# Two transposes of the identity in place of four at each settling place of a two-block transformer kernel

## The chip, the cores and the metric

The kernel runs on one core of one Trainium2 chip. The metric is the device time of one execution in microseconds, the median of the runs. All data are 32-bit floats; the large products are made with TensorE's fp32r type from operands that are split into a high and a low part.

## The reference, cut to what matters

One sequence of 256 tokens with 2048 channels passes two blocks. The first has a gated linear attention, a dilated window attention and a product-key expert layer; the second has a pooling layer and a linear recurrence, each with gates and an output projection.

```python
xn = rms_norm(x, norm1_g)
h = xn @ w_in                                  # then attention parts of h
x = x + mixed @ w_out
...
u = expert_down[ib]                            # first block: all 16384 experts, with gates
act = gelu(einsum('tkd,td->tk', u, xb))
x = x + einsum('tk,tkd->td', gb * act, expert_up[ib])
...
for i in range(2):                             # second block: pooling, then recurrence
    uz = rmsnorm(x, g_pre[i]) @ w_in[i]
    y = pool_mixer(u) or rglru(conv(u))
    o = (y * silu(z)) @ w_out[i]
    x = x + rmsnorm(o, g_post[i])
    gate = sigmoid(rmsnorm(x, g_ple_in[i]) @ w_ple_gate[i])
    x = x + rmsnorm((p[i] @ w_ple[i]) * gate, g_ple_out[i])
```

The kernel computes the expert layer densely: every expert's activation for every token, times a gate that is zero for the experts that a token didn't choose.

## The kernel before, in words

All weights come as 589 chunks of 128 x 2048 numbers (1 MB), in one written-out order. SyncE issues the load of each chunk into one of three raw buffers (RAW). ScalarE rounds a chunk to its high part (WH, L1050), VectorE subtracts to get the low part (WL, L1555). Both parts have three slots; a few chunks have extra ones (WX). The activations stand transposed and split in the same way, k-tile by k-tile, high part and low part, in A, M, CO, DD, P or Y.

TensorE works through the chunks in order. A chunk is 16 blocks of 128 x 128 weights. For each block the function `block` issues three matmuls of 256 columns, each with its own weight load: high weights times high activations (L558), high weights times low activations (L559), low weights times high activations (L560). The prediction calls these three a triple, and the 16 triples (48 matmuls) of a chunk a tile. A tile's 16 blocks are added in one half of a PSUM bank. The weight load of the next matmul runs while the current one streams.

The chunk numbers of the stages: 0 to 12 gated linear attention, 13 to 48 dilated attention, 49 to 64 output projection, 65 to 80 queries, 81 to 152 and 225 to 280 the first ("down") products of the experts, 153 to 224 and 281 to 336 the second ("up") products, 337 to 416 the pooling layer's inputs, 417 to 448 its output projection, 449 to 450 and 451 to 466 its gate, 467 to 538 the recurrence's inputs, 539 to 570 its output projection, 571 to 588 the last gate.

Other work for TensorE is put between triples by hand: transposes and products of the attention heads (among them L718 and L719, two 512-column products with ones; L726, two transposes; L742, four transposes), the score products and the index transposes of the top-k stage (L839, L847), the gate products (L857), and the sums over channels by a product with ones (`summed`, L599, L601, L604).

At 24 places TensorE also makes transposes of the identity matrix, L573, by the function `settle`. Their output goes to the upper half of the bank whose lower half the next tile will fill; nobody reads it. The set SETTLE names 22 of them by chunk: 53, 68, 84, 105, 119, 129, 138, 147, 150, 227, 229, 344, 346, 361, 381, 401, 458, 474, 486, 504, 522 and 580. There the transposes stand ahead of the tile's first triple, behind the waits for the bank and for the chunk's low part. The other two are in the output projections, ahead of the second tile of each (chunks 418 and 540).

Of the kernel before, what the change touches and what calls it, by code (L numbers as in the profile page):

```python
# [12 lines left out]
T = 256  # L13
# [70 lines left out]
def build(nc, d, out):  # L84
# [483 lines left out]

    def settle(e, b):

        for i in range(4):
            at = T + i % 2 * 128
            e.transpose(BANK[b][:, at:at + 128], IDENT[:, :], IDENT[:, :])  # L573

    def tile(e, c, x):

        wait_bank(e, c)
        e.wait_ge(s_lo, c + 1)
        if c in SETTLE:
            settle(e, bank[c])  # L580
        for b in range(16):
            ins = block(e, psum(c), c, b, x, b, b == 0, b == 15)
            if b == 15:
                ins.then_inc(s_used, 1)
            yield b
# [336 lines left out]
    def pe_oproj(e, l):  # L922

        c0, n = C_O[l], LEAD[l]
        for hf in range(2):
            for i in range(n):
                c = c0 + n * hf + i
                if hf == 0:
                    wait_bank(e, ("o", l, i))
                    if l and i == 4:  # L930
                        e.wait_ge(RA.sem, RA.at(("ig", 7)))
                e.wait_ge(s_lo, c + 1)
                if hf == 0 and i == 1:
                    settle(e, bank["o", l, i])
                for b in range(16):
                    if i == 0:
                        wait_y(e, l, 16 * hf + b)
                    ins = block(e, psum(("o", l, i)), c, b, Y, 16 * hf + b, hf == b == 0, hf == 1 and b == 15)
                ins.then_inc(s_used, 1)
        for i in range(n, 16):  # L940
            wait_bank(e, ("o", l, i))
            for hf in range(2):
                c = c0 + 2 * i + hf
                e.wait_ge(s_lo, c + 1)
                for b in range(16):
                    ins = block(e, psum(("o", l, i)), c, b, Y, 16 * hf + b, hf == b == 0, hf == 1 and b == 15)
                ins.then_inc(s_used, 1)
# [1454 lines left out]
```

## Time and profile before

| | before |
|---|---|
| time, median of 3 runs | 3403.35 us |
| lowest and highest run | 3401.82 and 3406.58 us |
| the profiled execution's span | 3399.5 us |
| median less span | 3.85 us |
| PE (matmuls) busy | 3377.7 us |
| DVE busy | 2285.7 us |
| ACT busy | 1663.9 us |
| L573, the transposes of the identity | 96 instructions |

The span is measured from the first to the last instruction of one profiled execution, the run's time is that of whole executions; a single time of the profiled execution beside its span was not recorded, so the median stands beside it. PE's busy time counts matmuls that overlap, so a share near 100% says that a matmul was always under way, not how many there were. How many triples begin in a stretch of time is to be read from the start times and the counts.

### The profile page before, as it was taken

To read this page: it belongs to the slowest core of one execution; us is meant where nothing else is said; L and a number is where in the kernel's file an instruction comes from. 1 tells how busy PE (TensorE), PEld (TensorE's weight loads), DVE (VectorE), ACT (ScalarE), POOL (GpSimd) and SP (SyncE) were. 2 spreads that over 40 slices of the span, in tenths; PEclk is the share of its full clock that TensorE was granted. 3 is DMA by queue.
4 is the path that set the end of the run, shared out by engine and by line. 5 is a ranking of instruction groups with operands and counts; after the bars stand their busy time and mean duration, and the time that the engine had idled before them with its cause. 6 is when DMAs were issued, how large, how long until landed. Compare 5 with 4: busy or idle time off the path is not lost.

```text
span 3399.5 us, 66556 instructions
## 1 busy us (share of the span) xinstructions
PE 3377.7 (99%) x29384; PEld 3355.2 (99%) x29384; DVE 2285.7 (67%) x3023; ACT 1663.9 (49%) x1789; POOL 134.9 (4%) x132
## 2 busy tenths in 40 slices
PE   9999999999999999999999999999999999999999
PEld 9999999999999999999999999999999999999998
DVE  5777679986655555555555577788646778787466
ACT  5545444455544344344444453333445677777455
POOL 0000000144400000000000000000000000000000
PEclk9999999999999999999999999999999999999999
DMA  6445455566676665655566645555554545555543
GB/s 253 159 140 186 176 214 186 187 217 210 217 237 219 216 220 206 230 189 196 198 214 221 207 173 207 190 195 186 199 199 176 200 162 199 199 181 192 204 181 137
DMA packets 125328, 669.45 MB, mean 197 GB/s; under 512 B 11056, under 2 KB 44592, under 8 KB 47344
## 3 DMA queue, kind: packets, MB, share of 16 engines
q1 hardware_dynamic: 88224, 623.44, 52.0%
q10 hardware_dynamic: 36816, 41.75, 3.7%
q8 instruction: 232, 3.80, 0.4%
q14 instruction: 56, 0.46, 0.0%
HBM read 643.39 MB, written 20.97 MB: 195 GB/s over the span
## 4 chain that ended last, share of the span: by engine, by line
PE 94%; DVE 3%; ACT 1%; issue 1%; DMA 0%; ACTq 0%; SPq 0%; DVEq 0%
PE PS L558 30%; PE PS L559 30%; PE PS L560 30%; PE PS L857 2%; DVE WL L1555 1%; ACT WH L1050 1%; DVE A L1579 0%; DVE WX L1555 0%; PE PS L573 0%; PE PS L748 0%; PE PS L733 0%; PE PS L839 0%; DVE OO L2100 0%; DVE XT L2106 0%; PE PS L701 0%
## 5 line engine op out<-in xcount | busy, mean ns | idle before, releaser
L1555 DVE TENSOR_TENSOR WL<-RAW,WH 128x2048 fp32r<-128x2048 f32 x576 | 1318.6, 2290 | 811.2 <-ACT WH L1050 809.0
L558 PE MATMUL PS<-A,WH 128*128 128x256 f32 x5536 | 1544.6, 279 | 7.4 <-DVE A L1579 5.1
L560 PE MATMUL PS<-A,WL 128*128 128x256 f32 x5536 | 1531.6, 277 | 0.0
L559 PE MATMUL PS<-A,WH 128*128 128x256 f32 x5536 | 1531.6, 277 | 0.0
L1050 ACT ACTIVATE WH<-RAW 128x2048 fp32r<-128x2048 f32 x576 | 1102.1, 1914 | 843.6 <-PE PS L560 830.5
L558 PEld LDWEIGHTS PS<-A,WH 128*128 128x128 f32 x5536 | 1041.8, 188 | 11.9 <-issue 4.4
L559 PEld LDWEIGHTS PS<-A,WH 128*128 128x128 f32 x5536 | 1040.3, 188 | 0.7
L560 PEld LDWEIGHTS PS<-A,WL 128*128 128x128 f32 x5536 | 1040.1, 188 | 0.0
L558 PE MATMUL PS<-CO,WH 128*128 128x256 f32 x2048 | 565.2, 276 | 0.0
L559 PE MATMUL PS<-CO,WH 128*128 128x256 f32 x2048 | 565.2, 276 | 0.0
L560 PE MATMUL PS<-CO,WL 128*128 128x256 f32 x2048 | 565.2, 276 | 0.0
L558 PEld LDWEIGHTS PS<-CO,WH 128*128 128x128 f32 x2048 | 384.4, 188 | 0.0
L559 PEld LDWEIGHTS PS<-CO,WH 128*128 128x128 f32 x2048 | 384.4, 188 | 0.0
L560 PEld LDWEIGHTS PS<-CO,WL 128*128 128x128 f32 x2048 | 384.4, 188 | 0.0
L558 PE MATMUL PS<-Y,WH 128*128 128x256 f32 x1152 | 318.1, 276 | 0.0
L560 PE MATMUL PS<-Y,WL 128*128 128x256 f32 x1152 | 318.0, 276 | 0.0
L559 PE MATMUL PS<-Y,WH 128*128 128x256 f32 x1152 | 318.0, 276 | 0.0
L1273 ACT ACTIVATE GA<-TMP 128x256 f32<-128x256 f32 x128 | 53.5, 418 | 374.8 <-DVE TMP L1746 374.8
L559 PEld LDWEIGHTS PS<-Y,WH 128*128 128x128 f32 x1152 | 216.3, 188 | 0.0
L558 PEld LDWEIGHTS PS<-Y,WH 128*128 128x128 f32 x1152 | 216.3, 188 | 0.0
L560 PEld LDWEIGHTS PS<-Y,WL 128*128 128x128 f32 x1152 | 216.3, 188 | 0.0
L1922 POOL TENSOR_SCALAR OB<-IOTA,I2T,GTT 128x128 f32<-128x128 f32 x128 | 134.8, 1064 | 802.1 <-ACT GTT L1294 642.1
(305 smaller groups left out, 2930.8 us busy)
## 6 DMA issues: line engine op xcount, KB each, us to landing
RAW<-in_w_in SPq DMA_DIRECT2D x175, 1024.0 KB, 4.8
RAW<-in_peer_down SPq DMA_DIRECT2D x128, 1024.0 KB, 4.8
RAW<-in_peer_up SPq DMA_DIRECT2D x128, 1024.0 KB, 5.3
RAW<-in_w_out SPq DMA_DIRECT2D x80, 1024.0 KB, 4.7
RAW<-in_w_gate SPq DMA_DIRECT2D x32, 1024.0 KB, 4.8
RAW<-in_w_query SPq DMA_DIRECT2D x16, 1024.0 KB, 4.8
gates_away<-XT ACTq DMA_DIRECT2D x16, 1024.0 KB, 8.1
RAW<-in_pool_w SPq DMA_DIRECT2D x16, 1024.0 KB, 4.8
```

The source lines that it names most:

```text
L558: e.matmul(ps, wh, x[:, k, 0, :], start=first, stop=False, skip_group_check=True)
L559: e.matmul(ps, wh, x[:, k, 1, :], start=False, stop=False, skip_group_check=True)
L560: return e.matmul(ps, wl, x[:, k, 0, :], start=False, stop=last, skip_group_check=True)
L857: ins = e.matmul(BANK[5 + q % 2][:, k * 128:k * 128 + 128], OA[:, q % 2, k, :], OB[:, q % 2, k, :], start=True, stop=True, skip_group_chec ...
L1050: e.activation(W_HIGH[c], RAW[:, c % NRAW, :], ACT.Copy).then_inc(s_hi, 1)
L1273: e.activation(GA[:, jj, :], TMP[:, n_gelu[p, jj] % 2, :], ACT.Gelu_apprx_tanh).then_inc(s_gelu, 1)
L1555: e.tensor_tensor(W_LOW[c], RAW[:, c % NRAW, :], W_HIGH[c].bitcast(F32), ALU.subtract).then_inc(s_lo, 1)
L1922: return e.tensor_scalar(OB[:, q % 2, k, :], IOTA[:, :], I2T[:, tok:tok + 1], GTT[:, tok:tok + 1], ALU.is_equal, ALU.mult)
```

## The change

`settle` issues two transposes, one into each quarter of the upper half of the bank, where it issued four, two into each quarter. The number of settling places, their positions and everything else stay.

```diff
     def settle(e, b):
 
-        for i in range(4):
-            at = T + i % 2 * 128
+        for at in (T, T + 128):
             e.transpose(BANK[b][:, at:at + 128], IDENT[:, :], IDENT[:, :])
```

## Rows read from the trace of the kernel before

**Rows 1.** The page: span, busy time and share by engine, granted clock in 40 slices

```profile
span 3399.5 us, 66556 instructions
...
PE 3377.7 (99%) x29384; PEld 3355.2 (99%) x29384; DVE 2285.7 (67%) x3023; ACT 1663.9 (49%) x1789; POOL 134.9 (4%) x132
...
PEclk9999999999999999999999999999999999999999
```

**Rows 2.** The chain that ended last, share of the span by engine

```profile
PE 94%; DVE 3%; ACT 1%; issue 1%; DMA 0%; ACTq 0%; SPq 0%; DVEq 0%
```

**Rows 3.** Groups by line and form, PE: count, busy us, mean ns, idle before

```profile
L573 PE MATMUL PS<-IDENT 128*128 128x128 f32 x96 | 14.4, 273 | 1.0 <-DVE WL L1555 1.0
```

**Rows 4.** Timeline at the settling place of chunk 129: start us, duration us

```profile
822.69 0.28 PE L560 MATMUL PS<-A,WL 128*128 128x256 f32 x1
...
823.03 0.28 PE L560 MATMUL PS<-A,WL 128*128 128x256 f32 x1
...
823.15 0.60 PE L573 MATMUL PS<-IDENT 128*128 128x128 f32 x4
...
823.50 0.37 PE L558 MATMUL PS<-A,WH 128*128 128x256 f32 x1
...
823.70 0.28 PE L559 MATMUL PS<-A,WH 128*128 128x256 f32 x1
...
823.82 0.28 PE L560 MATMUL PS<-A,WL 128*128 128x256 f32 x1
```

**Rows 5.** L560 in four stretches: duration ns min/median/max, first and last start us

```profile
L560 PE MATMUL PS<-A,WL x114: 281/281/281, 39.7 to 79.7; 128*128 128x256 f32 x114
...
L560 PE MATMUL PS<-M,WL x178: 276/276/276, 369.7 to 429.9; 128*128 128x256 f32 x178
...
L560 PE MATMUL PS<-A,WL x44: 281/281/281, 2736.1 to 2751.3; 128*128 128x256 f32 x44
...
L560 PE MATMUL PS<-A,WL x123: 276/276/276, 2752.8 to 2799.7; 128*128 128x256 f32 x123
```

**Rows 6.** Timeline at other transposes, and L560 in the stretches behind them

```profile
105.76 0.38 PE L726 MATMUL PS<-IDENT,QKV 128*128 128x128 f32 x2
...
L560 PE MATMUL PS<-A,WL x29: 276/276/277, 106.2 to 115.7; 128*128 128x256 f32 x29
...
340.61 0.38 PE L726 MATMUL PS<-IDENT,QKV 128*128 128x128 f32 x2
...
L560 PE MATMUL PS<-M,WL x3: 281/281/281, 341.1 to 341.8; 128*128 128x256 f32 x3
...
638.75 0.49 PE L847 MATMUL PS<-IDENT,IX 128*128 128x128 f32 x3
...
L560 PE MATMUL PS<-A,WL x26: 276/276/281, 639.3 to 647.8; 128*128 128x256 f32 x26
...
L560 PE MATMUL PS<-A,WL x13: 281/281/281, 303.6 to 307.9; 128*128 128x256 f32 x13
...
L560 PE MATMUL PS<-A,WL x17: 276/276/277, 323.3 to 328.8; 128*128 128x256 f32 x17
```

**Rows 7.** The last L560 ahead of settling places (chunks 129, 401, 105, 68)

```profile
L560 PE MATMUL PS<-A,WL x1: 280/280/280, 823.0 to 823.0; 128*128 128x256 f32 x1
...
L560 PE MATMUL PS<-A,WL x1: 280/280/280, 2337.8 to 2337.8; 128*128 128x256 f32 x1
...
L560 PE MATMUL PS<-A,WL x1: 283/283/283, 661.5 to 661.5; 128*128 128x256 f32 x1
...
L560 PE MATMUL PS<-A,WL x1: 281/281/281, 449.2 to 449.2; 128*128 128x256 f32 x1
```

**Rows 8.** Waits of PE: us in total, times, longest us

```profile
PE PS L573 <- DVE WL L1555: 1.0, 1, 1.0
```

## The prediction

> **What bounds the kernel now.** I read the head of the page and its busy shares first. TensorE's matmul row is busy for 3377.7 us of a span of 3399.5, VectorE for 2285.7, and the granted clock stands at nine tenths or more in every slice, which is the 2.4 GHz level [rows 1]. Then the chain that ended last: 94% of it is PE [rows 2]. So a nanosecond taken out of TensorE's stream is a nanosecond off the span, unless the next instruction has to wait for something else. All waiting of that kind is a few microseconds; at the settling places it is one wait of 1.0 us for VectorE's low half of a chunk [rows 8]. The median of the runs, 3403.35 us, lies 3.85 us above the profiled span. I carry that difference over unchanged.
>
> What I then want from the trace is not the share but the rhythm. The matmul stream is a triple (L558, L559, L560) repeated about 9,400 times, and the same L560 shows two rhythms [rows 5]. Between 369.7 and 429.9 us 178 of them start: 60.2/177 = 340 ns a triple, each lasting 276 ns. Between 39.7 and 79.7 us 114 start: 40.0/113 = 354 ns a triple, each lasting 281 ns. Later on 44 of them in 15.2 us give 353.5 ns, again at 281 ns, and right behind the settling place at 2752 us they are back at 276. Duration tells the pace: minimum, median and maximum are the same number in each stretch. I call them quick and slow. They differ by 13.4 ns a triple (3.9%), or 16 x 13.4 = 0.214 us for a tile of 48 matmuls. The granted clock is 1.0 in both, so this is no matter of the clock. Neither pace leaves by itself: slow lasts over 40 us in the first of these rows, quick over hundreds of microseconds. Something must interrupt the stream to change it. The places where four transposes stand are such interruptions; after all 24 of them the trace has 276 ns, also after the four that were entered at the slow pace (366, 449, 2752 and 3336 us).
>
> **What the change removes.** One settling place, step by step [rows 4]: the triple before starts its L560 at 823.03, the four transposes begin at 823.15 and the last of them ends 0.60 us later. One lasts 273 ns [rows 3], so three spacings fill 0.33 us: 0.109 us each. Two transposes less are 2 x 0.109 = 0.218 us, and 24 x 0.218 = 5.2 us. Nothing else starts or waits on these outputs; they land in the unused half of a PSUM bank. One place (chunk 346, where the wait of 1.0 us is) stands behind a wait for VectorE. The 0.218 us saved at the place before it, chunk 344, can vanish into that wait, and two more near the top-k stage may vanish too. The direct saving is between 21 and 24 times 0.218, 4.6 to 5.2 us; I take 5.2.
> The Trainium skill, page "TensorE: Matmul & The Clock Gate", section "Back-to-back issue gap", gives about 81 ns a matmul for 128 columns in a sustained stream. By it the 48 transposes would be worth an estimated 3.9 us instead of 5.2. The trace has 109 ns here, and the trace decides.
>
> **What the removed pair may have done.** The pace behind the interruption is the other half of the sum. The trace has no pair of transposes standing alone between triples, so I bound it by its neighbours [rows 6].
> - A pair behind two 512-column matmuls (L718, L719, then L726 twice) occurs twice without more behind it. At 105.76 us the stream was quick and stays quick (29 times 276 ns). At 340.61 us it was slow and stays slow (281 ns).
> - Three transposes alone (L847, at 638.75 us), entered quick: five late starts (the maximum of 281 ns), then quick.
> - The same pair with four more right behind it: entered quick it comes out slow (13 times 281 ns from 303.6 us on), entered slow it comes out quick (from 323.3 us on).
> So transposes as such don't restore the quick pace. What counts is where in the beat the first weight load behind them falls, and that depends on their number.
>
> Where does that load fall after two? The start times in nanoseconds (the timeline rounds them to ten) show that all quick stretches keep one beat of 6.67 ns, a seventeenth of the 113.3 ns spacing. I followed the weight load in this beat through the transposes of each place. There are two kinds of quick entry, and the duration of the last L560 ahead of the transposes names them [rows 7]: 280 ns at eight places (chunks 129, 147, 227, 344, 401, 458, 504 and the output projection of the second layer), 282 or 283 ns at eleven. After two transposes the eleven stand where the trio at 638.75 us stood after three, and that came out quick. The eight stand after two where the pair at 340.61 us stood: the next load at the same point of the beat, about one eighth of it past the point where the quick pace starts its matmuls. All three runs of transposes in the trace whose following load falls on that point (at about 140, 303 and 340 us) are followed by the slow pace. With four the eight places pass this point and come to another. The four slow entries stand after two near the point of the pair at 105.76 us, which came out quick; for chunk 68 there is no neighbour.
>
> **The sum.** Eight places come out slow until something else resets the pace: the next settling place, or a stage's end. In tiles of 16 triples that is 0.5 (129, up to the gate matmuls), 3 (147 to 150), 2 (227 to 229), 2 (344 to 346), 17 (401 to 418), 9 (458 to the sums of the first layer's end), 18 (504 to 522) and 31 (540 to 571): 82.5 tiles x 0.214 = 17.7 us. About 0.5 us comes back, because the ones-matmuls (L599, L601) that now throw a quick stream into the slow pace would meet a slow one. Net: 17.7 - 0.5 - 5.2 = +12.0 us, 3411.5 for the span and 3415.4 for the median.
> Bounds of this term: nothing, if the pair settles everywhere (-5.2 us); and all of the 8,500 quick triples slow (+114 us), which I do not believe, since slow entries have neighbours that turn quick.
>
> **The rivals.**
> *Two do what four do.* For it: 20 of the 24 places are entered quick, and none of the rows with an undisturbed quick entry (four, three) ends slow. Against it: the pair that stays slow at 340.61 us. Time: 3403.35 - 5.2 = 3398.2. A measurement of this kernel tells about 0.2% (6.8 us) from no change, so this rival is "the same". It decides as soon as fewer than some 8 tiles are slow in all.
> *The slow pace also gets into the long stretches.* The two kinds of entry need not keep their places once the stream before them has moved. Chunk 150 is followed by 75 tiles without a break, chunk 229 by 109 (up to the end of the second up stage): 16 and 23 us if one of them is entered wrongly, or if a slow stream from 147 or 227 passes through its pair. Time: 3415.4 + 16 to + 23 = 3431 to 3438, and 3454 with both. Against it: slow entries with a near neighbour in the trace come out quick.
> *More is won than the transposes.* For over 0.2% faster, 1.6 us more than the 5.2 must go, such as two of the slow stretches of some 40 triples behind the sums (0.5 us each) and part of the first one. Nothing in the edit touches what starts these; 3396 at best.
> *The edit is hidden.* TensorE would have to wait for the weights anyway. It waits once in 24 places, so no.
>
> **How the numbers follow.** Eight places slow, as in the sum: 0.45; its own range is 3405 to 3426 (half of the tiles; or four more stretches of 10 to 18 tiles). Long stretches slow as well: 0.19. Two do what four do: 0.32. More won than that: 0.04. The likeliest gives 3415. The range reaches down to the second rival and up to one long stretch: 3397 to 3440; beyond it lie the case with both long stretches and half of the last rival, under 0.15. Faster by over 0.2%: 0.04. Slower: 0.45 + 0.19 less 0.02 for a sum that stays under 3410 = 0.62. Within: 0.34.
>
> **What would show it.** L573 must appear 48 times at 273 ns, and a settling place must be shorter by 0.22 us. The matmul L560 between the settling places is the witness: 281 ns from 401's place (2338 us) to 418's, from 504's to 522's and from 540's to the end of that stage, 276 ns elsewhere. If it is 276 throughout, the pace argument is wrong and the time is 3398. If it is 281 between 970 and 1370 or between 1402 and 1990 us, the third case has come. A slow stretch behind a place whose last L560 took 283 ns, or a quick one behind 280, would say that the beat point was misread even if the total comes out right.

## The result and the profile after

| | before | after |
|---|---|---|
| median | 3403.14 us (4 runs) | 3439.39 us (4 runs) |
| lowest and highest | 3401.82 and 3406.58 | 3434.10 and 3441.38 |
| ratio, 95% interval | | 1.0101 [1.0088, 1.0113] |
| span of the profiled execution | 3399.5 us | 3432.8 us |

The kernel became 36 us slower by the medians, 33.3 us by the profiled spans. The change took out what it says, and lost seven times as much elsewhere.

The page of the kernel after, and its row for the transposes, answer to [rows 1 to 3]:

```profile
span 3432.8 us, 66460 instructions
...
PE 3412.2 (99%) x29336; PEld 3389.1 (99%) x29336; DVE 2287.1 (67%) x3023; ACT 1664.1 (48%) x1789; POOL 137.1 (4%) x132
...
PE 95%; DVE 3%; ACT 1%; issue 1%; DMA 0%; ACTq 0%; SPq 0%; DVEq 0%
...
L572 PE MATMUL PS<-IDENT 128*128 128x128 f32 x48 | 9.2, 273 | 1.2 <-DVE WL L1554 1.2
```

48 transposes fewer, VectorE and ScalarE as busy as before, and no new wait: the one ahead of a transpose is 1.2 us instead of 1.0. Shares and waits say nothing about where 33 us went. The duration of the third matmul of the triple does. These are the answers for L560 in six stretches of the kernel after (duration ns min/median/max, first and last start us); [rows 5] shows the same line before:

```profile
L560 PE MATMUL PS<-A,WL x247: 276/276/278, 449.8 to 540.7; 128*128 128x256 f32 x124
...
L560 PE MATMUL PS<-A,WL x313: 276/281/283, 543.3 to 653.4; 128*128 128x256 f32 x157
...
L560 PE MATMUL PS<-CO,WL x1103: 280/281/282, 989.4 to 1378.7; 128*128 128x256 f32 x184
...
L560 PE MATMUL PS<-CO,WL x832: 275/276/277, 1702.2 to 1984.7; 128*128 128x256 f32 x167
...
L560 PE MATMUL PS<-A,WL x247: 280/281/282, 2842.6 to 2940.8; 128*128 128x256 f32 x124
...
L560 PE MATMUL PS<-Y,WL x409: 281/281/282, 3140.5 to 3284.7; 128*128 128x256 f32 x137
```

In these six the slow pace fills the stretches behind chunks 84, 150, 486 and 540; behind chunk 401 it does too, with the lines of L560 from 2359.5 us on at a median of 281 ns:

```profile
L560 PE MATMUL PS<-A,WL x192: 280/281/282, 2359.5 to 2438.3; 128*128 128x256 f32 x192
```

Between 989.4 and 1378.7 us 1103 triples start: 389.3/1102 = 353.3 ns each; between 1702.2 and 1984.7 us 832 start at 340.0. Before the change the first of these stretches was quick:

```profile
L560 PE MATMUL PS<-CO,WL x1152: 276/276/276, 982.8 to 1374.1; 128*128 128x256 f32 x192
```

Counted over the whole trace by the distance from one triple's start to the next (340 against 353 or 354 ns), the kernel before has 632 slow triples and the kernel after 3538. (Distances that hold a wait or other work are not counted.) The difference, 2906 x 13.3 ns = 38.7 us, less 5.2 us for the 48 transposes, is 33.5 us; the spans differ by 33.3.

The timeline of the kernel after at the place that cost most, chunk 150 (start us, duration us), is to be set beside [rows 4], which shows chunk 129:

```profile
971.84 0.28 PE L560 MATMUL PS<-A,WL 128*128 128x256 f32 x1
971.96 0.38 PE L572 MATMUL PS<-IDENT 128*128 128x128 f32 x2
972.09 0.36 PE L558 MATMUL PS<-A,WH 128*128 128x256 f32 x1
972.29 0.28 PE L559 MATMUL PS<-A,WH 128*128 128x256 f32 x1
972.41 0.28 PE L560 MATMUL PS<-A,WL 128*128 128x256 f32 x1
972.53 0.28 PE L558 MATMUL PS<-A,WH 128*128 128x256 f32 x1
```

From the transposes to the next L558 it is 0.13 us where [rows 4] has 0.35: the 0.22 us saved are there. But behind it the steps are 0.12, not 0.11, and stay so for 1198 triples.

### The profile page after: what moved, and what is told of

The parts are those of the page before. It is cut to its first block, busy times and chain, and to the rows that moved or that the text cites. A ratio compares the mean times of both kernels' runs of the same rounds, so it can differ in the third digit from the quotient of the medians.

```text
span 3432.8 us, 66460 instructions
## 1 busy us (share of the span) xinstructions
PE 3412.2 (99%) x29336; PEld 3389.1 (99%) x29336; DVE 2287.1 (67%) x3023; ACT 1664.1 (48%) x1789; POOL 137.1 (4%) x132
## 4 chain that ended last, share of the span: by engine, by line
PE 95%; DVE 3%; ACT 1%; issue 1%; DMA 0%; ACTq 0%; SPq 0%; DVEq 0%
PE PS L558 30%; PE PS L559 30%; PE PS L560 30%; PE PS L856 2%; DVE WL L1554 1%; DVE A L1578 0%; ACT WH L1049 0%; DVE WX L1554 0%; PE PS L747 0%; PE PS L732 0%; PE PS L838 0%; DVE OO L2099 0%; DVE XT L2105 0%; PE PS L700 0%; DMA RAW<-in_w_in 0%
## 5 line engine op out<-in xcount | busy, mean ns | idle before, releaser
L558 PE MATMUL PS<-A,WH 128*128 128x256 f32 x5536 | 1551.9, 280 | 6.2 <-DVE A L1578 5.1
L560 PE MATMUL PS<-A,WL 128*128 128x256 f32 x5536 | 1538.9, 278 | 0.0
L559 PE MATMUL PS<-A,WH 128*128 128x256 f32 x5536 | 1538.8, 278 | 0.0
L558 PEld LDWEIGHTS PS<-A,WH 128*128 128x128 f32 x5536 | 1045.2, 189 | 11.1 <-issue 4.4
L560 PEld LDWEIGHTS PS<-A,WL 128*128 128x128 f32 x5536 | 1042.4, 188 | 0.0
L559 PEld LDWEIGHTS PS<-A,WH 128*128 128x128 f32 x5536 | 1040.9, 188 | 0.6
L558 PE MATMUL PS<-CO,WH 128*128 128x256 f32 x2048 | 571.4, 279 | 0.0
L559 PE MATMUL PS<-CO,WH 128*128 128x256 f32 x2048 | 571.4, 279 | 0.0
L560 PE MATMUL PS<-CO,WL 128*128 128x256 f32 x2048 | 571.4, 279 | 0.0
L559 PEld LDWEIGHTS PS<-CO,WH 128*128 128x128 f32 x2048 | 389.6, 190 | 0.0
L558 PEld LDWEIGHTS PS<-CO,WH 128*128 128x128 f32 x2048 | 384.6, 188 | 0.0
L560 PEld LDWEIGHTS PS<-CO,WL 128*128 128x128 f32 x2048 | 384.6, 188 | 0.0
L558 PE MATMUL PS<-Y,WH 128*128 128x256 f32 x1152 | 321.1, 279 | 0.0
L560 PE MATMUL PS<-Y,WL 128*128 128x256 f32 x1152 | 321.0, 279 | 0.0
L559 PE MATMUL PS<-Y,WH 128*128 128x256 f32 x1152 | 321.0, 279 | 0.0
L558 PEld LDWEIGHTS PS<-Y,WH 128*128 128x128 f32 x1152 | 218.7, 190 | 0.0
L559 PEld LDWEIGHTS PS<-Y,WH 128*128 128x128 f32 x1152 | 216.3, 188 | 0.0
L560 PEld LDWEIGHTS PS<-Y,WL 128*128 128x128 f32 x1152 | 216.3, 188 | 0.0
```

Of the source, the lines that this page charges most:

```text
L558: e.matmul(ps, wh, x[:, k, 0, :], start=first, stop=False, skip_group_check=True)
L559: e.matmul(ps, wh, x[:, k, 1, :], start=False, stop=False, skip_group_check=True)
L560: return e.matmul(ps, wl, x[:, k, 0, :], start=False, stop=last, skip_group_check=True)
```

## The experiments

Theory 1: an interruption of the stream leaves it in the quick or the slow pace by where in a short beat the next weight load falls, and the number of transposes moves that point. Theory 2: transposes pull the stream towards the quick pace, and more of them do so more surely. Theory 3, on the cause of the paces: they are two ways in which the reads of weights and of activations meet in memory, so the distance of their addresses decides what they cost. In the runs below `settle` takes its number of transposes from a function of the chunk, which the cuts show written out; all start from the kernel before. Its medians beside them were 3402.27 (first four), 3402.46 (next four) and 3403.57 us (last four). In these kernels the three matmuls of a triple are L559 to L561.

### Three everywhere

```diff
-        for i in range(4):
+        for i in range(3):
```

> Three transposes at all 24 places. Theory 1 (the number decides at which point of the beat the next weight load falls; each number has its own outcome by kind of entry): the trio of the index transposes in the kernel before, entered behind a matmul of 280 ns, came out quick after five late starts, and the places with two show quick for all nine slow entries; so three come out quick at every place whose entry is of the 280 kind, with five late starts each, and I expect quick nearly everywhere: 3403.1 - 24 x 0.109 = 3400.5 us, under 700 slow triples in all. Theory 2 (the more transposes, the surer the quick pace): between two and four, 3405 to 3425 us, with some of the long stretches slow.

Measured: 3404.61 us, ratio 1.0003 [0.9994, 1.0013]. No difference from the kernel before that can be told. It lies 4.1 us above theory 1's 3400.5 and 0.4 below the range that I gave theory 2, so it decides for neither. Theory 1's count was wrong: the profile (a span of 3406.5) has some 1,300 slow triples, not under 700, 318 of them behind chunk 361 and 286 behind 486, both entered quick behind a matmul of 282 ns. Each was put right at the next place. The places entered behind 279 to 281 ns all came out quick, as theory 1 had it.

### None anywhere

```diff
-        for i in range(4):
+        for i in range(0):
```

> No transposes of the identity at all. Theory 1: the pace changes only where something else interrupts. Slow from chunk 53 to the sums behind chunk 65 (205 triples more than before, 2.7 us), quick from there, because the sums turn the pace over, to about 1990 us; then as before up to chunk 474, slow from there to the sums near 3285 us (about 1550 triples, 20.7 us), quick for 40, and slow again or quick to the end. 3403.1 + 2.7 + 20.7 - 24 x 0.44 = 3416 us, with about 2,300 slow triples. Theory 2 (transposes pull towards the quick pace): without any, more stretches are slow than with two: above 3439 us.

Measured: 3458.12 us, ratio 1.0187 [1.0170, 1.0204], with single executions from 3431.80 to 3469.39. My 3416 was wrong, and theory 2's "above 3439 us" came true. The profile has 4486 slow triples where I had expected 2,300: the gate matmuls near 659 us also turned a quick stream slow, which they never did in the kernel before, and so did the product with ones at 2009 us. A hundred microseconds of it, each triple at 281 ns:

```profile
L561 PE MATMUL PS<-A,WL x252: 281/281/281, 2999.9 to 3099.9; 128*128 128x256 f32 x126
```

### Four at the four places entered slow, none elsewhere

```diff
-        for i in range(4):
+        for i in range(4 if c in (53, 68, 474, 580) else 0):
```

> Four transposes only at the four places that the kernel before enters slow (chunks 53, 68, 474, 580), none at the other twenty. Theory 1: a quick stream that nothing interrupts stays quick, so the twenty places did nothing: 3403.1 - 20 x 0.44 = 3394.3 us, some 650 slow triples as before. Theory 2 (the settling is also needed to keep the quick pace, which decays or is lost at other interruptions): some long stretches slow, 3405 us or more.

Measured: 3427.52 us, ratio 1.0071 [1.0033, 1.0109], 3414.36 to 3448.61. Wrong again by the 33 us between it and 3394, and the profile (a span of 3437.5) shows two large reasons. The stream doesn't decay (in the profiles no stretch changes its pace without an interruption), but other interruptions than in the kernel before turn it. One is a wait for weights with no transposes behind it:

```profile
2033.63 0.28 PE L561 MATMUL PS<-A,WL 128*128 128x256 f32 x1
2035.34 0.36 PE L559 MATMUL PS<-A,WH 128*128 128x256 f32 x1 [1.44 <-DVE WL L1556]
2035.53 0.28 PE L560 MATMUL PS<-A,WH 128*128 128x256 f32 x1
2035.65 0.28 PE L561 MATMUL PS<-A,WL 128*128 128x256 f32 x1
...
L561 PE MATMUL PS<-A,WL x865: 280/281/282, 2041.0 to 2425.4; 128*128 128x256 f32 x173
```

This stretch goes on to 2619.5 us, 1652 triples in all. The other begins behind a sum over channels (L605) at 2755 us: the four transposes at chunk 474 find the stream slow and leave it slow, for 1557 more triples. In the kernel before the same four brought it back.

So the twenty places that the kernel before enters quick are not idle as a group. At one of them, chunk 346, a wait of 1.0 us stands ahead of the transposes in the kernel before, and there the stream came out quick. Reading one trace, I had taken its quick entries for given.

### Two at chunk 150 alone

```diff
-        for i in range(4):
+        for i in range(2 if c == 150 else 4):
```

> Two transposes at chunk 150 alone, four at the other 23. In the kernel before this place is entered quick behind a matmul of 283 ns; in the changed kernel it was entered quick behind one of 282 ns and came out slow for 1198 triples. Theory 1a (the pair itself puts this kind of entry into the slow pace, as in the changed kernel): slow from 966 to about 1370 us, + 16.0 - 0.2: 3419 us. Theory 1b (my blind reading: this kind comes out quick, and in the changed kernel something else differed in the entry): no slow triples there, 3402.9 us.

Measured: 3418.10 us, ratio 1.0043 [1.0031, 1.0054]. Ten executions fall into two groups: 3402.20 and 3402.78, and eight from 3416.49 to 3422.05. One pair of transposes less costs 16 us, in eight of ten. The profiled execution is one of the two cheap ones, so no trace shows where the eight lost their 16 us; that it was behind chunk 150 is inferred from the price, which is that of 1198 triples at 13.3 ns:

```profile
L561 PE MATMUL PS<-CO,WL x1152: 276/276/276, 982.8 to 1374.1; 128*128 128x256 f32 x192
```

So 1a and 1b are both right, each in its share of the executions, as far as that inference holds. Two traces show both outcomes: a pair at chunk 150, entered quick behind a matmul of 282 ns, came out quick here and slow in the changed kernel.

### Two at the eight places of the prediction

```diff
-        for i in range(4):
+        for i in range(2 if c in (129, 147, 227, 344, 401, 458, 504, 540) else 4):
```

> Two transposes at the eight places that the prediction named (chunks 129, 147, 227, 344, 401, 458, 504, 540), four at the other sixteen. Theory 1, as in the prediction's sum: all eight come out slow until the next place restores the quick pace, 17.7 us of slow pace less 0.5 and less 8 x 0.218: 3402.3 + 15.5 = 3417.8 us, some 1,900 slow triples in the profile. Theory 2 (the place doesn't matter, a pair fails at random): about 3402 to 3410, with some of the eight quick.

Measured: 3406.77 us, ratio 1.0010 [1.0000, 1.0020], eleven executions, ten of them from 3403.91 to 3408.62 and one, the profiled, at 3431.18. Not the 3417.8 of the prediction's sum; the median lies in the range of theory 2. The profile, though it is of the dear execution, shows how five of the eight places come out quick (147, 227, 401, 458 and 540) and that it isn't by chance. At chunk 129 the last matmul ahead of the pair takes 280 ns, and the stretch behind is slow; at chunk 147 the next of the eight is now entered behind one of 282, and is quick:

```profile
L561 PE MATMUL PS<-A,WL x2: 276/278/280, 822.9 to 823.2; 128*128 128x256 f32 x2
...
L561 PE MATMUL PS<-A,WL x9: 281/281/283, 823.8 to 826.6; 128*128 128x256 f32 x9
...
L561 PE MATMUL PS<-A,WL x2: 276/279/282, 950.3 to 950.6; 128*128 128x256 f32 x2
...
L561 PE MATMUL PS<-A,WL x46: 276/276/281, 951.2 to 966.5; 128*128 128x256 f32 x46
```

The kind of entry belongs not to the place but to what came before. (The dear execution lost some 23 us behind chunk 229, where four transposes failed: 1744 triples at 281 ns. And the stretch behind chunk 129 was slow for 126 triples, not for the 8 up to the gate matmuls that the prediction's sum has: the slow pace passed the gate matmuls and lasted to the next settling place.)

### Two at the four places entered slow

```diff
-        for i in range(4):
+        for i in range(2 if c in (53, 68, 474, 580) else 4):
```

> Two transposes only at the four places entered slow (chunks 53, 68, 474, 580), four at the other twenty. Theory 1: a slow stream comes out of a pair quick, as at nine of nine places of the changed kernel: 3402.3 - 0.9 = 3401.4 us, the slow triples as in the kernel before (about 630). Theory 2 (a pair leaves the pace as it is): 3402.3 + 2.7 + 2.5 + 1.9 = 3409 us or more.

Measured: 3401.27 us, ratio 0.9999 [0.9989, 1.0008]. As theory 1 has it: all four come out quick in the profile. That saves 0.9 us by the count of transposes, which no measurement here can tell. The same profile has 772 slow triples where I had expected 630, because four transposes at chunk 458, entered slow, failed there.

### Other distances between weights and activations

```diff
     A = put("A", [128, KD, 2, T], FR)
-    place["at"] += 64
+    place["at"] += 128
```

> Four transposes as before; the raw, high and low weight buffers lie 64 bytes further on, so that weights and activations are 128 instead of 64 bytes apart within 1024. Theory 3 (the two paces are two ways in which the reads of weights and of activations meet in memory, and this distance decides their price): another price of the slow triple than 353.3 ns, or none. Rival: the paces don't depend on addresses, 340.0 and 353.3 ns as before, and about 3402 us.

> As the run before, with 320 bytes instead of 64 between weights and activations within 1024. Theory 3: another price of a triple in one of the paces, so that 340.0 or 353.3 ns changes. Rival: both as before, about 3402 us.

The distances are those of the start addresses within a partition, taken modulo 1024 bytes. The edit moves the three weight buffers and the small ones behind them, among them the ones and the identity; the activations stay.

Measured, one execution each (the second run has 320 in the place of 128): 3536.68 us at 128 bytes and 3401.28 at 320. L561 in the same stretch of the kernel at 128 bytes, then at 320 (the kernel before has 178 such starts in 60 us at the quick pace as well, [rows 5]):

```profile
L561 PE MATMUL PS<-A,WL x168: 279/281/285, 1439.8 to 1499.7; 128*128 128x256 f32 x168
```

```profile
L561 PE MATMUL PS<-A,WL x178: 276/276/276, 1439.8 to 1499.9; 128*128 128x256 f32 x178
```

At 128 bytes the quick pace is gone: 85 triples in the whole trace take under 345 ns, and the others spread from 351 to 361 (356.5 on average between neighbours in this stretch). At 320 bytes, which is 64 plus 256, both paces are back at 340 and 353 ns, and so are their places. So theory 3's expectation came true at 128 bytes and failed at 320; a period of 256 bytes would reconcile the two, and this pair alone speaks for it.

### 192 and 96 bytes, without transposes

```diff
-        for i in range(4):
+        for i in range(0):
...
-    place["at"] += 64
+    place["at"] += 192
```

> No transposes of the identity, and the weight buffers a further 128 bytes on: 192 instead of 64 bytes between weights and activations within 1024. At 64 and 320 the two triples took 340.0 and 353.3 ns, at 128 nearly none took 340. Theory 3 (the distance within 256 bytes decides which meetings cost something): 192 differs from both; if the slow pace is free there, 3402.3 - 24 x 0.44 - 630 x 0.0133 = 3383 us and no slow triples; if it is as 64, about 3458 us like the run without transposes; if it is as 128, over 3500 us. I hold the second for the likeliest (0.5), then the third.

> No transposes of the identity, 96 bytes between weights and activations. Same three outcomes as the run at 192: 3383, about 3458 or over 3500 us. Halfway between the distance with a quick pace (64) and the one without (128) I expect triples between 340 and 354 ns or a third pace, over 3458 us.

Measured: 3480.65 us at 192 (ratio 1.0221 [1.0200, 1.0241]) and 3511.11 at 96 (1.0315 [1.0275, 1.0354], two executions; its edit has 96 in the place of 192). The time at 192 is none of the three outcomes: it lies about halfway between 3458, which I had held for the likeliest, and 3500. The profile is of its slowest execution, 3498.89 us. At 192 the slow triple is the known one of 353.3 ns and 336 of 9,327 are quick; at 96 they spread from 350 to 363 with 62 quick ones. In the same stretch as above, 192 first:

```profile
L561 PE MATMUL PS<-A,WL x171: 280/280/280, 1439.7 to 1499.8; 128*128 128x256 f32 x171
```

```profile
L561 PE MATMUL PS<-A,WL x169: 277/281/283, 1440.0 to 1499.8; 128*128 128x256 f32 x169
```

At none of the distances tried is the slow pace as short as the quick one. Zero wasn't tried. Nor was the other way to move them apart: in all these runs the weights moved and the activations stayed, so the place of the weights by itself, and not their distance from the activations, may be what counts.

### The changed kernel with four at chunk 150

```diff
-        for i in range(4):
+        for i in range(4 if c == 150 else 2):
```

> The changed kernel with four transposes at chunk 150 alone, two at the other 23. Its profile had 1198 slow triples behind that place. Theory 1: they go, 3439.4 - 16.0 + 0.2 = 3424 us. Rival: the kinds of entry shift behind the place, and another long stretch (chunk 229, 1742 triples) turns slow more often: 3430 us or more.

Measured: 3436.76 us, ratio 1.0103 [1.0080, 1.0126]. The time is the rival's, its place is not: chunk 229 came out quick, and the profile is slow behind chunk 150 all the same, behind four transposes. Entered behind 23 other places with two each, four is no guarantee:

```profile
971.91 0.60 PE L574 MATMUL PS<-IDENT 128*128 128x128 f32 x4
...
972.27 0.36 PE L559 MATMUL PS<-A,WH 128*128 128x256 f32 x1
...
L561 PE MATMUL PS<-CO,WL x1106: 281/281/281, 989.5 to 1380.0; 128*128 128x256 f32 x185
```

### Six everywhere

```diff
-        for i in range(4):
+        for i in range(6):
```

> Six transposes at all 24 places. Theory 1 (the outcome depends on the number, not on there being enough): some places come out slow, above 3402.3 + 24 x 0.218 = 3407.5 us by the slow triples, 3410 to 3440. Theory 2 (four or more always settle): quick everywhere, 3407.5 us, about 630 slow triples.

Measured: 3436.10 us, ratio 1.0110 [1.0077, 1.0143]. Six are as bad as two. The direct cost is 5.2 us; the profile has 2776 slow triples. Theory 2 falls here: more transposes don't settle more surely. In the page of this run's trace, chunk 68 is entered slow and left slow, and chunk 150 entered quick and left quick:

```profile
L561 PE MATMUL PS<-A,WL x253: 281/281/282, 450.8 to 547.0; 128*128 128x256 f32 x127
...
L561 PE MATMUL PS<-CO,WL x1142: 276/276/276, 991.9 to 1379.8; 128*128 128x256 f32 x191
```

### All places of ten profiles together

Counted in the profiles of the kernels before and after and of the runs above with distances of 64 or 320 bytes (without chunk 346, which is entered behind a wait): how many places came out quick, and how many slow. The kind of a quick entry is read from the last matmul of the triple ahead of the transposes, as in [rows 7]. Below, the 280 kind is the table's second column and the third kind its third.

| transposes | quick entry, 278 to 281 ns | quick entry, 282 ns or more | slow entry |
|---|---|---|---|
| 2 | 1 quick, 17 slow | 11 quick, 3 slow | 25 quick, 1 slow |
| 3 | 7 quick, 0 slow | 6 quick, 2 slow | 8 quick, 0 slow |
| 4 | 32 quick, 0 slow | 47 quick, 2 slow | 21 quick, 5 slow |
| 6 | none seen | 11 quick, 0 slow | 6 quick, 6 slow |

From a quick entry a pair is far worse than four. From a slow entry the order is a pair, four, six; but 25 of 26 against 21 of 26 is a small difference, and these places aren't independent draws: a place sets the entry of the next, and the profiles of the changed kernel and of the one with four at chunk 150 run alike up to that chunk. The row of the pair holds what the change broke: 17 of 18 in its first cell, 3 of 14 in its second.

The distance in time from the weight loads ahead to the first weight load behind the transposes tells more than the duration does. I count it from the load of the last L559 (its place taken from seven loads, so as to get below the whole nanosecond). Of the 32 pairs entered quick, 21 have 450.3 to 452.7 ns, and 20 of them are followed by the slow pace; 11 have 453.0 to 453.7, and all are followed by the quick one. The failures of three and four lie in the gap between the two kinds as well: with three at 561.4 and 561.9 ns, between places at up to 560.4 and from 562.0 on that came out quick; with four at 670.3 and 671.0, between up to 669.7 and from 671.0 on.

## Why the prediction was right in direction and short in size

The median after, 3439.39 us, lies 0.6 us inside the upper end of the range, 3440, and far above the likeliest case's 3415 and its own range up to 3426. The profiled span rose by 33.3 us where the sum has 12.0.

**What bounds the kernel.** Right. TensorE's stream sets the time, and 33.5 us worked out from its triples meet 33.3 us of span.

**The direct saving.** Right: 48 transposes, 0.22 us a place in the timeline, 273 ns each. It was only inferred in the sum, since no run changed the transposes without changing the paces; the run with two at the four slow entries lies within what can't be told.

**The price of the slow pace.** Right: 13.3 ns a triple, foretold with 13.4.

**What a pair does.** Right for each kind of entry, as the table has it: the 280 kind comes out slow (17 of 18), slow entries come out quick (25 of 26), and the third kind mostly quick (11 of 14). The reading came from three neighbours in one trace and held over the five profiles that have pairs. But the prediction named a sign against itself, a slow stretch behind a place whose last L560 took 283 ns or a quick one behind 280, and the first came: chunk 138 was entered behind 283 and was slow. (The nearest to the second is chunk 361, entered behind 278 and quick.) What stands of the beat is that the point where the next weight load falls goes with the outcome; the duration of the last L560 names it only roughly. For chunk 138, the last L560 ahead (the second of two in this answer) and the stretch behind:

```profile
L560 PE MATMUL PS<-A,WL x2: 276/280/283, 891.3 to 891.7; 128*128 128x256 f32 x2
...
L560 PE MATMUL PS<-A,WL x143: 281/281/282, 892.2 to 954.9; 128*128 128x256 f32 x143
```

These are the sizes behind the 33.3 us, in slow triples of the profile after:

| | in the sum | in the profile |
|---|---|---|
| behind places of the 280 kind | 1,320 | 1681 (seven places) |
| behind places of the third kind | 0 | 1326 (chunks 150 and 138) |
| elsewhere, against before | 0.5 us less | 101 fewer |

At 13.3 ns the first row is 22.4 us instead of 17.7 and the second 17.6 instead of nothing.

**The third kind: here the sum failed.** The sum had the eleven places at nothing. Three of 14 came out slow over all profiles, and in the profile after two of six: chunk 150 with 1198 triples, 16 us, and chunk 138 with 128. The run with two at chunk 150 alone puts the chance there at eight in ten, if its eight dear executions lost their time there. This is the mechanism of the rival "the slow pace also gets into the long stretches", which I had priced at 3431 for one such stretch and given 0.19; the median came at 3439. Its sign came too: L560 at 281 ns from 989 to 1379 us. So the likeliest case had the direction and one part of the mechanism; the rival had the other part, which is where the size was short. The prediction's argument against that rival (slow entries come out quick) held, but it wasn't the way in: the entry was quick.

**Which places are of which kind.** The step "Eight places come out slow until something else resets the pace", 82.5 tiles or 1,320 triples, took the kinds from the trace of before as if they belonged to the places. After the change seven places were entered behind 280 ns: chunks 84, 105, 119, 227, 401, 486 and 540, three of them on my list. That so many, and with stretches as long, came out slow as on the list is luck. Of the three slow stretches that the prediction named as witnesses, those behind 401 and 540 were slow, and the one from 504's place to 522's (2943.7 to 3041.6 us) was quick.

The step "0.5 (129, up to the gate matmuls)" was wrong as well. A slow stream passes the gate matmuls: behind chunks 105, 119 and 138 it lasted 175, 142 and 128 triples, where 8 stand ahead of them. That is most of the excess in the table's first row.

The runs showed the wandering of the kinds once more from the other side: with two transposes at my eight places and four elsewhere the median is 3406.8, not 3417.8, because the first pair already changes the kind of the next entry. The kind depends on the interruptions before; what in them sets it stays open.

**Two do what four do.** Wrong: with its 3398 us it lies outside all executions.

**How paces and executions vary.** My working took the outcome of a place for fixed. Executions of the same program, the one with a pair at chunk 150, fall into two groups 16 us apart. One trace shows one draw, and I should have widened the likeliest case's own range for that.

**Why two paces at all.** Where the weights lie in memory, with the activations left in place, decides whether a quick pace exists: 64 and 320 bytes between them have it, 128 and 96 have nearly none, and 192 has few triples of it. That the reads of the two meet is a theory that fits; no run looked at the memory itself or moved the activations, so the cause is argued, and only the dependence on the addresses is shown. The Trainium skill says in "TensorE: Matmul & The Clock Gate", section "Step-by-step: what each phase is for", that loading the next tile's weights doesn't take read bandwidth from the running matmul. No run here shows what the reads do to each other, but the time does depend on where the weights lie: 3401.28 us at 320 bytes and 3536.68 at 128.

## What to carry to other kernels

Where a stream of matmuls with a weight load each bounds a kernel, measure its spacing in every stretch, not its busy share: a median duration that steps from 276 to 281 ns was the only sign of a loss of 39 us. Instructions that compute nothing may hold such a spacing; change them one place at a time and look at many executions, for a profile shows one draw. And ahead of any tuning of that kind place the weight and activation buffers against each other, since a shift by 64 bytes cost more here (134 us by one execution) than all of the settling gives (56 us).

## What the runs showed of the hardware that I had not expected

The spacing of the triples is bistable: 340.0 or 353.3 ns over more than a thousand triples, at a granted clock of 1.0 in both, and changed only by an interruption. Behind a quick entry of the 280 kind the outcome is nearly fixed by the number of transposes (2: 17 of 18 slow; 4: 32 of 32 quick); elsewhere it is not (6: quick in 6 of 12 from a slow entry). A difference of about a nanosecond in where the next weight load falls (452.7 against 453.0 ns) goes with the two outcomes of a pair. Offsets of 64 and 320 bytes between the two operands behave alike, 96, 128 and 192 each in a way of its own.
